# The convolution's first tap on ScalarE, its rows evenly spaced, gating work spread, and some loads and stores issued in another order

## The reference, cut to what matters

```python
y_a = spatial_gating_mixer(a_u, a_v, ...)       # gelu(u) * (W @ layernorm(gelu(v)) + b), chunks of 128 tokens
qkv = silu(causal_depthwise_conv([q, k, v], conv_w))   # mixer B: 4 taps, 12 blocks of 128 channels x 1024 tokens
q, k = l2norm(q), l2norm(k)                     # then gates, decays, products within chunks, a triangular solve
y_c = dilated_attention_mixer(c_q, c_k, c_v, rel_bias)
merged = sum_i sigmoid(gate_i) * (y_i @ w_branch_i);  x = x + merged @ w_out
```

## Time and profile before

| | us |
|---|---|
| median of 3 runs | 1921.72 (1921.02 to 1923.36) |
| the profiled execution | 1921.67 |
| its span, first to last instruction | 1919.9 |
| TensorE busy in the span | 1832.2 (95%) |
| VectorE, ScalarE, GpSimd busy | 1348.0, 1052.6, 328.9 |
| mean granted TensorE clock | 0.982 of full speed |

### The profile page before, as it was taken

The page is one execution under the profiler, slowest core; times in us unless marked ns, Lnnn a source line. Parts: engine busy times, 40 slices in busy tenths (PEclk is TensorE's granted clock), DMA queues, the critical chain, the costliest instruction groups (busy, mean ns, idle before and its releaser), DMA issues.

```text
span 1919.9 us, 27083 instructions
## 1 busy us (share of the span) xinstructions
PE 1832.2 (95%) x9326; PEld 1536.9 (80%) x9326; DVE 1348.0 (70%) x1799; ACT 1052.6 (55%) x1555; POOL 328.9 (17%) x493
## 2 busy tenths in 40 slices
...
GB/s 236 117 72 105 110 159 218 235 356 320 171 145 213 165 205 162 208 127 197 220 249 214 347 173 151 69 235 292 385 377 390 394 398 385 390 386 387 372 205 268
DMA packets 185131, 470.77 MB, mean 245 GB/s; under 512 B 29567, under 2 KB 59215, under 8 KB 183500
## 3 DMA queue, kind: packets, MB, share of 16 engines
...
q0 software_dynamic: 28960, 77.04, 12.0%
...
## 4 chain that ended last, share of the span: by engine, by line
PE 68%; DMA 3%; DVE 3%; SPq 1%; ACT 1%; issue 1%; POOL 0%; DVEq 0%; POOLq 0%; ACTq 0%
PE psum L735 18%; PE psum L737 18%; PE psum L736 18%; PE psum L2665 2%; PE psum L2642 2%; PE psum L3017 1%; DMA w_blk<-in_w_blocks 1%; DVE e_l L2400 1%; PE psum L2652 1%; PE psum L2797 1%; PE psum L2941 1%; PE psum L3039 1%; PE psum L3077 1%; PE psum L3078 1%; DMA br_l<-branch_low_scratch 1%
## 5 line engine op out<-in xcount | busy, mean ns | idle before, releaser
L2400 DVE TENSOR_TENSOR e_l<-e_raw,e_h 128x2048 fp32r<-128x2048 f32 x190 | 424.0, 2286 | 32.5 <-ACT e_h L1606 32.2
L735 PE MATMUL psum<-hf_h,wf_l 128*128 128x512 f32 x952 | 384.4, 404 | 31.2 <-DVE stage L1767 17.9
L737 PE MATMUL psum<-hf_h,wf_h 128*128 128x512 f32 x952 | 374.8, 394 | 0.0
L1606 ACT CAST e_h<-e_raw 128x2048 fp32r<-128x2048 f32 x190 | 355.0, 1925 | 35.6 <-DMA e_raw<-in_w_e 31.0
L736 PE MATMUL psum<-hf_l,wf_h 128*128 128x512 f32 x952 | 374.3, 393 | 0.0
L1737 DVE TENSOR_TENSOR wf_l<-w_blk,wf_h 128x512 fp32r<-128x512 f32 x238 | 163.5, 689 | 199.8 <-ACT wf_h L1266 199.3
L735 PEld LDWEIGHTS psum<-hf_h,wf_l 128*128 128x128 f32 x952 | 181.2, 190 | 71.0 <-issue 29.0
L1266 ACT CAST wf_h<-w_blk 128x512 fp32r<-128x512 f32 x238 | 147.1, 622 | 162.1 <-PE psum L737 139.6
L737 PEld LDWEIGHTS psum<-hf_h,wf_h 128*128 128x128 f32 x952 | 180.6, 190 | 39.4
L736 PEld LDWEIGHTS psum<-hf_l,wf_h 128*128 128x128 f32 x952 | 181.2, 190 | 34.7
L735 PE MATMUL psum<-e_h,xT_l 128*128 128x512 f32 x512 | 202.2, 395 | 1.4 <-DVE xT_l L2406 1.4
...
## 6 DMA issues: line engine op xcount, KB each, us to landing
...
```

The costliest lines, as they stand in the source:

```text
L735: nc.tensor.matmul(out_ap, ll, rh, start=first, stop=False, skip_group_check=goes_on)
L737: return nc.tensor.matmul(out_ap, lh, rh, start=False, stop=last, skip_group_check=goes_on)
L1606: nc.scalar.copy(e_h[:, c], e_raw[:, c]).then_inc(s_eh13 if c < 4 else s_eh2, 1)
L2400: nv.tensor_tensor(e_l[:, c], e_raw[:, c], e_h[:, c].bitcast(F32), ALU.subtract).then_inc(s_el13 if c < 4 else s_el2, 1)
```

## The change: what it does

The first tap of each convolution row is now a ScalarE copy with a per-channel scale (`conv_first`), issued in the slots g = 2 and g = 3 of each chunk; VectorE keeps the three multiply-adds, now always at the end of slots g = 0 and g = 2. Gating products come every second slot (30, 32, ... 44) instead of every slot, the norms in slots 25 to 29 instead of 25 to 32, the split of y_a in slots 49, 53, 55, 57. The 24 branch splits stand in slots 12 to 27 (every third), 32 to 47 (every fifth) and 54 to 93 (every third), and the next raw block is loaded right behind a split, after the store of the block before, issued two slots or more earlier. Small math moves to slots 48 and 53 to 59. On SyncE, `early_loads(1)` stands behind the four weight blocks; two of the four delta tiles of the next to last chunk stand behind its `stage` stores. On GpSimd, six of the twelve first loads of queries and keys stand behind the values' loads.

The diff, cut where it only repeats:

```diff
--- before.py
+++ after.py
@@ -33,7 +33,7 @@
 PT_ROWS = (N_CHUNK - CH_QK) * CW
 ROW_Z, ROW_GATE = (CH_Z - CH_QK) * CW, (CH_GATE - CH_QK) * CW
 BIAS_SLOT, A_SQ_SLOT, A_NORM_SLOT, A_SV_SLOT, SMALL_SLOT, EARLY_SLOT, SOLVE_SLOT, C_SLOT = 9, 20, 25, 30, 48, 61, 83, 82
-SMALL_DVE, SMALL_ACT = (0, 2, 4, 7, 9, 11), (0, 3, 8)
+SMALL_DVE, SMALL_ACT = (0, 6, 7, 9, 10, 11), (5, 6, 9)
 TURN_SLOT, FIRST_P5, FIRST_X5, FIRST_P6 = N_SLOT - 4, N_SLOT - 3, N_SLOT - 2, N_SLOT - 1
 N_FORM = 7
 N_PAIR = N_CHUNK - CH_U
@@ -65,6 +65,16 @@
 def added(x, i):
 
     return 3 * x + ADDED[i]
+
+
+def conv_started(n):
+
+    return 4 * (n // 2) + n % 2 + 1
+
+
+def conv_activated(n):
+
+    return conv_started(n) + 2
 
 
 def turn_step(j):
@@ -121,7 +131,9 @@
 N_ROWS = 20
 ROW_Q, ROW_QD, ROW_GC, ROW_RK, ROW_KB = 0, 4, 8, 12, 16
 SB = 32
-SPLIT_SLOT, SPLIT_EVERY, YA_SLOT = 12, 3, 44
+YA_SLOTS = (49, 53, 55, 57)
+SPLITS = tuple(range(12, 28, 3)) + tuple(range(32, 48, 5)) + tuple(range(54, 94, 3))
+NORMS = {A_NORM_SLOT: (0,), A_NORM_SLOT + 1: (1, 2), A_NORM_SLOT + 2: (3,), A_NORM_SLOT + 3: (4, 5), A_NORM_SLOT + 4: (6, 7)}
 SOLVE_STEPS = 3
 LA_ROW, LA_TILE = 2 * 4 * P, 2 * 4 * P * P + P
 DI_ROW, DI_TILE = 4 * P, 4 * P * P + P
@@ -790,7 +802,6 @@
                 sp.wait_ge(s_yast, 32 * NH)
                 sp.dma_start(e_mask[:], b_masks[:, 1:2]).then_inc(s_emk, 16)
                 early_loads(0)
-                early_loads(1)
 
             def diagonal_blocks():
                 for u in range(2):
@@ -839,6 +850,8 @@
                     early_loads(2 * k + 1)
                 if CH_U <= c < N_CHUNK - 1:
                     weight_blocks(c - CH_U + 1, (3,))
+                if k == 0:
+                    early_loads(1)
                 if 0 <= k < NT // 2:
                     early_stored(2 * k)
                 if c == chunk_group(SOLVE_SLOT)[0]:
@@ -852,11 +865,13 @@
                     sp.wait_ge(s_xst, 16 * NH)
                     for u in range(2):
                         sp.wait_ge(s_eo[u], 16 * NT // 2)
-                    for t in range(NT // 2):
+                    for t in range(2):
                         delta_tile(t)
                 if c == N_CHUNK - 1:
                     sp.wait_ge(s_grp, PLAIN_GROUPS + N_FORM * (N_PAIR - 1) + 1)
                     sp.dma_start(b_lev[:], b_masks[:, LEVELS:LEVELS + 2]).then_inc(s_lev, 16)
+                    for t in range(2, NT // 2):
+                        delta_tile(t)
                 if c >= CH_QK:
                     stored(2 * (c - CH_QK) + 1)
                 if 0 <= k and k + 1 < NT // 2:
@@ -1090,7 +1104,7 @@
                     keys_queries(0, 0)
                 if h:
                     table(h)
-                keys_queries(h, 1)
+                    keys_queries(h, 1)
                 if h == 0:
                     lower_stored(NT - 1)
                     for u in range(2):
@@ -1101,6 +1115,8 @@
                     for u in range(2):
                         pool.wait_ge(s_la[u], 16 * NT // 2)
                 dilated_values(h)
+                if h == 0:
+                    keys_queries(0, 1)
                 if h:
                     rows_stored(8 * h - 1)
                     rows_loaded(h - 1)
@@ -1316,11 +1332,24 @@
                     act.wait_ge(s_asq, t)
                 nc.scalar.activation(ps[6], av[:, t], ACT.Square, bias=a_sum[:, t:t + 1], accum_out=a_sq[:, t:t + 1]).then_inc(s_asq, 1)
 
+            def conv_first(n):
+                row, x = n ^ 1, CH_B - CH_U + n // 2
+                act.wait_ge(s_ed, added(x, 1 if n % 2 else 5))
+                if n % 2:
+                    act.wait_ge(s_ev, copied(x, 6))
+                if n < 2:
+                    act.wait_ge(s_frd, 16)
+                    act.wait_ge(s_bload, 64)
+                else:
+                    act.wait_ge(s_cvst[n % 2], 16 * (n // 2))
+                    act.wait_ge(s_bsq, min(n - 1, NQ))
+                nc.scalar.activation(co[:, n % 2], stage[:, row % RING], ACT.Copy, scale=b_cw[:, row, 3:4]).then_inc(s_bsilu, 1)
+
             def conv_silu(n):
                 act.wait_ge(s_bconv, n + 1)
                 nc.scalar.activation(co[:, n % 2], co[:, n % 2], ACT.Silu).then_inc(s_bsilu, 1)
                 if n < NQ:
-                    act.wait_ge(s_bsilu, n + 1)
+                    act.wait_ge(s_bsilu, conv_activated(n))
                     if n >= 2:
                         act.wait_ge(s_bss, n - 1)
                     nc.scalar.activation(b_sq[:, n % 2], co[:, n % 2], ACT.Square).then_inc(s_bsq, 1)
@@ -1460,6 +1489,8 @@
                     evacuate(n)
                 elif g < 3:
                     product_out(N_FORM * (c - CH_U) + 2 * g + 1)
+                if g > 1 and 0 <= 2 * (c - CH_B) < NCONV:
+                    conv_first(2 * (c - CH_B) + g - 2)
                 if n == T_SLOT + 4:
                     for i in range(3):
                         h_form_high(i)
@@ -1477,19 +1508,18 @@
                     group_weights(j // 8 - 1)
                 if 8 <= j and phase == 1 and turn_step(j) in (0, 1):
                     rows_turned(j // 8 - 1, turn_step(j))
-                if n == SPLIT_SLOT - 2:
+                if n == SPLITS[0] - 2:
                     raw_branch(0)
                     raw_branch(1)
-                m, step3 = (n - SPLIT_SLOT) // SPLIT_EVERY, (n - SPLIT_SLOT) % SPLIT_EVERY
-                if 0 <= m < 3 * KD:
-                    if step3 == 0:
-                        branch_split(m)
-                    elif step3 == 1:
-                        branch_stored(m)
-                    elif m + 2 < 3 * KD:
-                        raw_branch(m + 2)
-                if YA_SLOT <= n < YA_SLOT + 2 * NH and (n - YA_SLOT) % 2 == 0:
-                    y_a_high((n - YA_SLOT) // 2)
+                if n in SPLITS:
+                    m = SPLITS.index(n)
+                    branch_split(m)
+                    if 0 < m < 3 * KD - 1:
+                        raw_branch(m + 1)
+                if n - 1 in SPLITS:
+                    branch_stored(SPLITS.index(n - 1))
+                if n in YA_SLOTS:
+                    y_a_high(YA_SLOTS.index(n))
                 if A_SQ_SLOT <= n < A_SQ_SLOT + NT // 2:
                     v_squares(2 * (n - A_SQ_SLOT))
                     v_squares(2 * (n - A_SQ_SLOT) + 1)
@@ -1843,18 +1873,9 @@
                 nv.tensor_tensor(o, ps[2 + n % 4], o, ALU.mult).then_inc(s_ay, 1)
 
             def conv(n):
-                row, x = n ^ 1, CH_B - CH_U + n // 2
-                dve.wait_ge(s_ed, added(x, 1 if n % 2 else 5))
-                if n % 2:
-                    dve.wait_ge(s_ev, copied(x, 6))
-                if n < 2:
-                    dve.wait_ge(s_frd, 16)
-                    dve.wait_ge(s_bload, 64)
-                else:
-                    dve.wait_ge(s_cvst[n % 2], 16 * (n // 2))
-                    dve.wait_ge(s_bsq, min(n - 1, NQ))
+                row = n ^ 1
+                dve.wait_ge(s_bsilu, conv_started(n))
                 raw, o = stage[:, row % RING], co[:, n % 2]
-                cd.link(nv.tensor_scalar(o, raw, b_cw[:, row, 3:4], None, ALU.mult))
                 for d in range(1, 4):
                     ins = nv.scalar_tensor_tensor(o[:, d:T], raw[:, 0:T - d], b_cw[:, row, 3 - d:4 - d], o[:, d:T], ALU.mult, ALU.add)
                     if d < 3:
@@ -2050,8 +2071,6 @@
                 j, phase = (n - C_SLOT) // 2, (n - C_SLOT) % 2
                 p = N_FORM * (c - CH_U) + 2 * g
                 k = n - first_slot(CH_B) - 2
-                if g == 0 and k >= 0 and k % 2 == 0 and k // 2 < NCONV:
-                    conv(k // 2)
                 if c >= CH_U:
                     product_added(p)
                 if phase == 0 and 0 <= j + 1 < 8 * NH and (j + 1) % 8:
@@ -2091,12 +2110,12 @@
                     v_means()
                 if n == A_SQ_SLOT + NT // 2:
                     v_roots()
-                if g and k >= 0 and k % 2 == 0 and k // 2 < NCONV:
+                if k >= 0 and k % 2 == 0 and k // 2 < NCONV:
                     conv(k // 2)
-                if A_NORM_SLOT <= n < A_NORM_SLOT + NT:
-                    v_normalized(n - A_NORM_SLOT)
-                if A_SV_SLOT + 1 <= n < A_SV_SLOT + 1 + 2 * NH:
-                    y_gated(n - A_SV_SLOT - 1)
+                for t in NORMS.get(n, ()):
+                    v_normalized(t)
+                if A_SV_SLOT < n < A_SV_SLOT + 4 * NH and (n - A_SV_SLOT) % 2:
+                    y_gated((n - A_SV_SLOT) // 2)
                 if n - SMALL_SLOT in SMALL_DVE:
                     small_math(SMALL_DVE.index(n - SMALL_SLOT))
                 if n >= EARLY_SLOT and (n - EARLY_SLOT) % 2 == 0:
...
```

22 lines of the change are left out of this document (10 added, 12 removed).

## The result

| | before | after |
|---|---|---|
| median, us | 1922.54 (1921.02 to 1926.96, 4 runs) | 1900.08 (1899.54 to 1902.41, 4 runs) |
| the profiled execution, its span | 1921.67, 1919.9 | 1902.41, 1900.3 |
| PE busy | 1832.2 (95%) | 1826.3 (96%) |
| mean granted clock | 0.982 | 0.985 |

A forecast was written before the change was run, and what follows sets the result against it. PE is busy 95% of the span, so only its gaps and the slow-clock products behind them can be won. 8 + 4.5 + 5.5 + 6.5 - 1 = 23.5 us off 1921.7 gives 1898 us, range 1886 to 1911.

The forecast's parts named there:

- A: Convolution, 180 to 330 us: 8 of 16.2 us of gaps and slow product go; bounds 0 and 15.
- The chunk's sum: Convolution chunk from 0: odd block ends at 11.4, copy at 12.0; 0.9 us spare with square sums, 1.0 late without.
- the rule that a gap of up to 3.02 us costs only itself: PE's gaps: up to 3.02 us no slow product follows; from 3.88 us on a gap costs itself and 2.5 us.
- no copy would idle over 1 us for `co`: Expected profile sign, 180 to 330 us: ScalarE's copies no longer idle for the convolution above 1 us each.
- The multiply on ScalarE: Convolution: 12 added multiplies at 1.06 us, 12.7 us in all, hidden in ScalarE's waits for PE, cost 0.
- B: 356 to 482 us: weight block 3 can come at most 4.6 us sooner by bytes; 4.5 us won, bounds 1 and 10.5.
- rival (1): Weight-block waits at 356 to 482 us are bytes, not order: only 1 and 1.5 us won there, 1906 us; chance 0.20.
- C: Gap at 481.83: six key and query loads, 1.5 MB, come later; 5.5 us won, bounds 1.5 and 8.
- my own signs of being wrong: Convolution gaps above 12 us, DMA share under 0.9 where PE awaits weights, or new gaps before first attention products or delta stage.
- D: Last chunk, 926.03: the gap of 3.97 us and its slow product go; 6.5 us won, bounds 5 and 7.
- E: Four branch splits beside the solve, slots 84 to 93: 1 us lost, bounds 0 and 2.8.

The follow-up runs named there:

- u_branch: Changed kernel with branch splits on every third slot from 12 to 81 again and raw blocks loaded two slots behind a split; 1909.73 us, ratio 0.9934.
- u_early: Changed kernel with the second big early load in front of the weight blocks again; 1906.42 us, ratio 0.9905.
- u_tap: Changed kernel with the first tap back on VectorE, directly in front of the three multiply-adds at their new place; 1910.07 us, ratio 0.9930.
- u_keys: Changed kernel with the six key and query loads of the second half in front of the values' loads again; 1906.10 us, ratio 0.9903.
- b_tap: Kernel before the change with only the first tap on ScalarE and the odd convolution block at the end of slot g = 0; 1919.92 us, ratio 0.9981.
- v_keys: Changed kernel with first six key/query loads behind the early stage's last store, other six behind attention's first row store; 1902.09 us, ratio 0.9887.

## Why the prediction was right, step by step

**A, the convolution: 8 forecast, 8.3 measured.** The total is right partly by luck. I forecast 8 of 16.2 us by 330; there 10.6 are won, and 2.4 are lost between 327 and 343. The chunk's sum holds within 0.5 us: in the chunk that starts at 277.25 the odd block is over 11.7 us later (11.4 forecast), the copy 12.4 (12.0), and the two chunks without square sums both have a gap (1.38 and 2.01 us, forecast 1.0). The four with square sums have none above 0.51 us. The small math was put at about 4 with what clock it costs; its new slots cost 2.4 us after 330 (the distance of kernels with old and new slots between 327 and 343 us). The part that I had not priced here is the branch split that leaves slot 33: undone with the other splits (u_branch) it is worth 4.0 us of this stretch. What failed is the rule that a gap of up to 3.02 us costs only itself. It came from too few rows, and 2.01, 1.11 and even 0.47 us were followed by a slow product. Of the profile I had said that no copy would idle over 1 us for `co`; it idles 5.6 us in a chunk, 33.6 in all, and PE pays for it only in the gaps above, 4.2 us in all.

**The multiply on ScalarE:** priced at 1060 ns, it takes 1154. The Trainium skill's "ScalarE: Activation LUTs", What ACT_TABLE_LOAD costs, led to an estimate of 1.13 us; the trace's 1.154 agrees. The Rules for kernel authors of the same page of the Trainium skill put a `mul` on VectorE. For the operation alone the rows agree (748 ns there, 1154 on ScalarE); for this kernel they do not: with the tap back on VectorE it is 7.8 us slower.

**B, 343 to 440 us: 4.5 forecast, 5.4 measured.** The size is near, the limit behind it is not shown. I had said that by the bytes the block at 452.20 can come at most 4.6 us sooner whatever the order; it assumed that the stretch begins when it did, while the changed kernel reaches it 8.3 us sooner and that product starts 13.9 us sooner. Bytes do count: taking 5.4 MB out gives 2.8 us by 440 and 6.1 by 491. Order counts as well: my rival (1), that it does not matter there, fell with u_early, whose order alone is worth 6.9 us (4.4 by the ratio). The 5.4 is also a net figure: the gap that stood at 377 gives 7.1 us by the product that the changed kernel starts at 367, 4.6 are lost by 399, with new gaps at 378 and 391, and 3.0 are won again by 440.

**C, 440 to 515 us: 5.5 forecast, 0.0 measured.** This is the step that failed: before minus after is 13.7 at 440 us and 13.7 at 491. The forecast was 4.4 us of gap for 1.5 MB out of the way, and 1.1 for a clock that stays up. The gap shrinks by 2.0 us (5.49 to 3.49), the slow product behind it stays, and the six moved loads meet the next chunk's first block: 6.66 us on ScalarE, a new gap of 1.51 us on PE at 491.15. SyncE issues the weight block that is waited for at these times, before and after:

```profile
467.36 0.33 SPq L758 DMA_DIRECT2D w_blk<-in_w_blocks  x1
```

```profile
453.44 0.33 SPq L770 DMA_DIRECT2D w_blk<-in_w_blocks  x1
```

VectorE reads it at 479.60 and 463.68, so 12.2 and 10.2 us after the issue. Each time the issue stands 2.0 us behind GpSimd's first key load (465.44 and 451.44). It follows the products, so that the kernel arrives 13.7 us sooner does not crowd the block: u_branch and u_tap arrive over 9 us later than the changed kernel and have 11.0 and 10.5 us. With twelve loads of keys and queries it takes 12.2 (before), 13.7 (u_keys) and 13.9 us (b_tap), with six 9.9 to 11.9 (seven kernels), and in v_keys, with none, 5.6. My reading of the rows was wrong in one point: the six moved loads did not stand in front of the block. The first of them is issued 1.3 us behind it in the kernel before:

```profile
468.66 0.55 POOL L1008 DMA_DIRECT2D c_q<-pt_scratch  x1
```

So they only share the DMAs with it, and 1.5 MB cost it 2 to 3.5 us instead of 4.4; why the kernel before has the least of the three times with twelve stays open. One of my own signs of being wrong came true here: the share of DMA is 0.85 between 440 and 490 us, under 0.9, while PE still waits for weights.

**D, the last chunk: 6.5 forecast, 6.9 measured** (20.7 - 13.8), undone 5.1.

**E, splits beside the solve: -1 forecast, 0.1 measured.** From 491 to 894 us the distance stays within 0.1 us.

The terms of the sum give 8.3 + 5.4 + 0 + 6.9 + 0.1 = 20.7 by the profiles up to 917 us; the spans differ by 19.6 (where the other 1.1 is lost was not looked into) and the medians by 22.5. So the terms are 2.8 us below the 23.5: C's 5.5 too many, less 2.7 by which A, B, D and E are above theirs. That the medians differ by 22.5, near 23.5, is luck: the changed kernel's profiled execution is 2.3 us above its median, and before's 0.9 below. The parts are not additive: undone one at a time they cost 5.1 + 6.9 + 4.4 + 8.5 + 7.8 + 1.1 = 33.8 us, while all together gave 20.7. The small math is not in that sum, and the spreading of the gating and of the y_a split was not tried alone.
